# Four chunks of each layer's input weights, split by DMA and ScalarE in place of ScalarE and VectorE

## The chip, the cores and the metric

The kernel runs on one core of a Trainium2 chip. The metric is the device time of one execution in microseconds (us). In the text PE is TensorE, DVE is VectorE, ACT is ScalarE, POOL is GpSimd and SP is SyncE; us counts from the start of the profile's span.

## The reference

Two layers of a hybrid encoder over 512 tokens of width 1024, in float32, and a final RMSNorm.

```python
D_MODEL = 1024; SEQ = 512; DEPTH = 2
D_IN = 4 * NA_W + 4 * DIL_W + 3 * CONV_CH        # 3712 = 29 x 128
def hybrid_layer(x, g, w_in, rpb, w_dw, b_dw, ln_g, ln_b, w_pw, b_pw, w_out, pos):
    h = rms_norm(x, g)
    z = h @ w_in
    aq, ak, av, ag, bq, bk, bv, bg, ca, cb, cg = jnp.split(z, splits, axis=-1)
    ya = neighbourhood_attention(heads(aq), heads(ak), heads(av), rpb) * silu(ag)
    yb = dilated_attention(rotary(heads(bq)), rotary(heads(bk)), heads(bv)) * silu(bg)
    yc = conformer_conv(ca, cb, w_dw, b_dw, ln_g, ln_b, w_pw, b_pw) * silu(cg)
    return x + concatenate([ya, yb, yc]) @ w_out
```

What the change touches is the product h @ w_in: how the weights get on chip in the form that it wants.

## The kernel before

**Products in three parts.** Each float32 factor is split into a high part rounded to fp32r and a low part, the remainder. A product is a_hi w_hi + a_hi w_lo + a_lo w_hi, so three matmuls of 128x128 by 512 for each slice of 128 of the contraction. One 128-wide column tile of the weights is a chunk: [128, 8, 128], 512 KB, 24 matmuls (`products`, L476 to L490).

**Chunks.** A layer has 40 chunks: 29 of w_in in the order of IN_TILES (L47), 3 of w_pw with 3 slices only, 8 of w_out. Chunks 0 to 8 (PRE = 9, L56) come before the attention units, namely cb0, bq0, ca0, bk0, cb1, ca1, bq1, cb2, bk1; "cb", "ca" are the convolution's inputs, "bq", "bk" the queries and keys that get rotary embedding. From chunk 9 on, PE does half a chunk in each of the 40 attention units (an eighth of a pair of heads each), beside their scores, transpositions and value products. w_hi and w_lo have SPL = 5 slots; chunk c lies in slot c % 5, which is free when tile c - 5 is done.

**Two ways to get w_hi and w_lo.** `by_engines(c)` (L68) chooses.

- By engines (before: chunks 0 to 8): SP loads the chunk raw into one of 4 buffers inside pT (`load`, L387), ACT copies it to w_hi, which rounds (`split_hi`, L702), DVE subtracts w_hi from the raw chunk into w_lo (`split_weights`, L1202). PE waits for lo_ready.
- By transfers (all others): POOL issues a load that casts into w_hi (`load_hi`, L915), ACT writes the negative of w_hi to w_lo (`negate`, L695), and POOL issues the same load again with an adding transfer onto w_lo (`load_lo`, L921), so that w_lo = w - w_hi. PE waits for the semaphore of that transfer.

In the text a "casting load" is `load_hi`, an "adding load" is `load_lo`, and a pair is one of each.

**The order on the engines.** Everything is written out by hand. While PE works on chunk c, POOL issues the casting load of chunk c + 4 (`hi_next`, CAST_AHEAD) and the adding load of c + 3 (`lo_next`, AHEAD), ACT splits or negates chunk c + 3 (`split_next`), DVE splits c + 3 (`weights_next`), SP loads raw chunk c + 7 (`load_next`). An engine that waits holds up all that is queued behind it.

**Rotary.** For tiles bq and bk DVE writes the scaled tile to zs (in sq), SP swaps its halves with four small DMAs of 64 KB each (`swap`, L407, the "swap" of the text; swap 0 is chunk 1's, swap 1 chunk 3's, swap 2 chunk 6's), POOL multiplies by the sines (`rotate`, L950), DVE adds (`rotated`, L1080), ACT rounds q_hi or k_hi (L778), DVE makes q_lo or k_lo. On POOL `rotate` of chunk c - 1's tile stands behind `hi_next` and `lo_next` of step c (L967 to L971).

**The norm.** The RMS factor comes late: column sums on PE (L547), mean on DVE, the reciprocal root on POOL (`root`, L945), spread by PE (L556). The first tile is emptied only then.

**The units.** In unit n ACT does: empty the transposed tile of unit n - 3 (L787), exponential of unit n (L762), scaling of n - 1 (L769), and for even n `split_next`. PE's transposition of unit n - 2 (L590) waits until ACT has emptied the one before (pt_ready).

```python
for n in range(SLOTS):
    if n > LAG:
        empty_turn(l, n - LAG - 1)
    if n < UNITS:
        exps(l, n)
    if 0 < n <= UNITS:
        norm(l, n - 1)
    if n < UNITS:
        if n % 2 == 0:
            split_next(l, tile_at(n)[0])
```

Of the kernel before, what the change touches and what calls it, by code (L numbers as in the profile page):

```python
# [55 lines left out]
PRE = 9  # L56
# [3 lines left out]
SPL = 5  # L60
RAW = 4
AHEAD = SPL - 2
CAST_AHEAD = SPL - 1
RAW_AHEAD = AHEAD + RAW
# [1 line left out]


def by_engines(c):  # L68
    return c < PRE


PAIRS = 5
# [52 lines left out]
def build(nc, xT, w_in, w_pw, w_out, prm, gfin, nabias, lncnt, rope, out):  # L125
    with ExitStack() as ctx:
# [161 lines left out]
        def nth(l, c):  # L288

            return sum(by_engines(d % N_CH) == by_engines(c) for d in range(N_CH * l + c + 1))  # L290
# [4 lines left out]
        def follows(l, c):  # L295

            l, c = (l, c) if c < N_CH else (l + 1, c - N_CH)
            return (l, c) if l < DEPTH else None
# [11 lines left out]
        def emptied(l, c):  # L310

            return ACC0 + N_CH * l + c + 1
# [12 lines left out]
        def rope_of(c):  # L325
            kind, j = IN_TILES[c]
            return 2 * j + (kind == "bk") if kind in ("bq", "bk") else None
# [22 lines left out]
        def tile_at(n):  # L350

            return PRE + n // 2, n % 2 == 1
# [17 lines left out]
        def blocks(g):  # L370
            return (u if g else cs)[:, :, :].rearrange("p j t -> p (j t)")
# [13 lines left out]
        @block.sync  # L385
        def _(sp):
            def load(l, c):  # L387
                m = nth(l, c) - 1
                if l and c < RAW:

                    sp.wait_ge(tile_done, N_CH * (l - 1) + N_IN + CT + c + 1)
                elif m == RAW:
                    sp.wait_ge(w0_lo, len(W0_PARTS))
                elif m > RAW:
                    sp.wait_ge(lo_ready, m - RAW)
                sp.dma_start(raw[:, m % RAW, :, :], w_in[l, c]).then_inc(raw_in[m % RAW], 16)

            def load_next(l, c):
                f = follows(l, c + RAW_AHEAD)
                if f is not None and by_engines(f[1]):  # L400
                    load(*f)

            def load_first(i):
                part = slice(*W0_PARTS[i])
                sp.dma_start(raw[:, 0, part, :], w_in[0, 0][:, part, :]).then_inc(w0_in[i // 2], 16)

            def swap(l, r):  # L407

                sp.wait_ge(acc_free, emptied(l, IN_TILES.index(("bk" if r % 2 else "bq", r // 2))))
                for h in range(4):  # L410
                    o = 32 * (h ^ 1)
                    sp.dma_start(zsw[32 * h:32 * h + 32, :], zs[o:o + 32, :]).then_inc(swap_in, 16)

            def move_x(g, first, end):
                ks = list(X_BLOCKS.values())[g]
                sp.wait_ge(x_blocks, ks[-1] + 1)
                to = x[:, ks[0]:ks[-1] + 1, :].rearrange("p k (a t) -> p (k a) t", t=P)
                turned = blocks(g)[:, 0:len(ks) * SEQ].rearrange("p (b t) -> p b t", t=P)
                for i, j in QUADS[first:end]:
                    sp.dma_start(to[32 * j:32 * j + 32, :, 32 * i:32 * i + 32],  # L420
                                 turned[32 * i:32 * i + 32, :, 32 * j:32 * j + 32]).then_inc(x_moved, 16)

            def load_bias(l, un):
                b = un - DUNITS

                sp.wait_ge(m_ready, UNITS * l + (un - 1 if b >= 2 else DUNITS - 4))
                sp.dma_start(bias[:, b % 2, :], nabias[l, b]).then_inc(bias_in[b % 2], 16)

            sp.dma_start(par[:, :], prm[0]).then_inc(par_in, 16)
            for i, k in enumerate(K_ORDER):  # L430
                if i in W0_PARTS:
                    load_first(i)
                sp.dma_start(x[:, k, :], xT[:, k, :]).then_inc(x_in[k], 16)
            load(0, 1)
            load(0, 2)
            sp.dma_start(cs[:, :, :], rope).then_inc(const_in, 16)
            load(0, 3)
            sp.dma_start(cnt[:, :], lncnt).then_inc(const_in, 16)
            for c in range(RAW, RAW_AHEAD):
                load(0, c)  # L440
            for l in range(DEPTH):
                for c in range(PRE):
                    if (r := rope_of(c)) is not None:
                        swap(l, r)
                    load_next(l, c)
                if l == LAST:
                    sp.dma_start(gf[:, :], gfin).then_inc(gf_in, 16)
                for n in range(UNITS):
                    c, ends = tile_at(n)
                    if ends and (r := rope_of(c)) is not None:  # L450
                        swap(l, r)
                    if n == DUNITS - 4:
                        load_bias(l, DUNITS)
                        load_bias(l, DUNITS + 1)
                    if DUNITS <= n < UNITS - 2:
                        load_bias(l, n + 2)
                    if l == LAST and n in X_MOVES:
                        move_x(*X_MOVES[n])
                if l == LAST:
                    move_x(2, 2 * (UNITS - 37), len(QUADS))  # L460
                if l + 1 < DEPTH:

                    sp.wait_ge(ylo_ready, KD * (l + 1))
                    sp.dma_start(par[:, :], prm[l + 1]).then_inc(par_in, 16)
                for c in range(N_IN, N_CH):
                    load_next(l, c)
            for a in range(QT):
                sp.wait_ge(res_act, a + 1)
                sp.wait_ge(res_dve, a + 1)
                sp.dma_start(out[a, :, :], res[:, 2 * a:2 * a + 2, :]).then_inc(out_in, 16)  # L470
            sp.wait_ge(out_in, 16 * QT)
# [442 lines left out]
        def _(pool):  # L914
            def load_hi(l, c):  # L915
                src, K = chunk_src(l, c)
                if N_CH * l + c >= SPL:
                    pool.wait_ge(tile_done, N_CH * l + c - SPL + 1)
                pool.dma_start(w_hi[:, c % SPL, 0:K, :], src).then_inc(whi_in[c % SPL], 16)  # L919
# [6 lines left out]
            def hi_next(l, c):  # L926
                f = follows(l, c + CAST_AHEAD)
                if f is not None and not by_engines(f[1]):
                    load_hi(*f)

            def lo_next(l, c):
                f = follows(l, c + AHEAD)
                if f is not None and not by_engines(f[1]):
                    load_lo(*f)
# [10 lines left out]
            def root(l, k):  # L945

                pool.wait_ge(misc_free, MISC_L * l + k + 1)
                nc.gpsimd.tensor_tensor(rcol[:, :], col[:, :], nhalf[:, :], ALU.pow).then_inc(pow_ready, 1)
# [11 lines left out]
                                    pattern=[[-1, P]], channel_multiplier=1).then_inc(consts, 1)  # L960
            for l in range(DEPTH):
                if l == 0:
                    pool.wait_ge(const_in, 32)
                else:
                    add_squares(l, KD - 1)
                root(l, MISC_COL)
                for c in range(PRE):  # L967
                    hi_next(l, c)
                    lo_next(l, c)
                    if c and (r := rope_of(c - 1)) is not None:  # L970
                        rotate(l, r)  # L971
                for n in range(UNITS + 1):
                    if n < UNITS and n % 2 == 0:
                        hi_next(l, tile_at(n)[0])
                    if n < UNITS and n % 2 == 1:
                        lo_next(l, tile_at(n)[0])
                    if n % 2 and (r := rope_of(tile_at(n - 2)[0])) is not None:
                        rotate(l, r)
                    if n == LN_SUM:

                        pool.wait_ge(conv_step, STEPS * (l + 1))
                        for j in range(1, CT):
                            a = y[:, KD - CT, :] if j == 1 else ssq[:, :]
                            nc.gpsimd.tensor_tensor(ssq[:, :], a, y[:, KD - CT + j, :], ALU.add).then_inc(add_done, 1)
                            pool.wait_ge(add_done, ADD_L * l + KD - 1 + j)
                    if n == LN_MEAN + 1:
                        for j in range(1, CT):
                            add_squares(l, j, base=1)
                    if n == LN_BC - 2:
                        root(l, MISC_LCOL)  # L990
                for c in range(N_IN, N_CH):
                    hi_next(l, c)
                    lo_next(l, c)
                    if c >= N_IN + CT + 2 and l < LAST:
                        add_squares(l + 1, c - (N_IN + CT) - 1)
# [448 lines left out]
```

## Time and profile before

| what | value |
|---|---|
| median of 3 runs | 542.46 us (540.92 to 544.98) |
| the profiled execution | 542.2 us, of which the span of the profile is 540.2 us |
| PE busy | 528.5 us (98%) |
| DVE, ACT, POOL busy | 361.1, 287.3, 135.3 us |
| instructions | 7426 |
| DMA traffic | 86.26 MB, mean 160 GB/s |

The span goes from the first instruction to the last; the 2.0 us around it are the start and the end of the execution. Busy shares are means over the whole span. PE's matmuls overlap in the records, so a matmul "lasts" 390 ns but the next starts 227 ns after it.

### The profile page before, as it was taken

What the parts mean: (1) busy time and instruction counts of PE and PEld (TensorE: products, weight loads), DVE (VectorE), ACT (ScalarE), POOL (GpSimd) and SP (SyncE); (2) the same over time, 40 slices, a digit from 0 to 9 for tenths busy, and PEclk for the clock granted to TensorE, in tenths of its full rate; (3) what the DMA queues carried; (4) which work ended last, traced back from release to release, by engine and by line L of the source; (5) the groups of instructions that cost most, each with busy time, mean ns of one, the idle gap of its engine ahead of it and who ended that gap; (6) DMA issues with size and microseconds to landing.
All of it is one profiled execution on the core that took longest, in us unless ns stands there. A gap on an engine that the chain in (4) does not pass through costs nothing.

```text
span 540.2 us, 7426 instructions
## 1 busy us (share of the span) xinstructions
PE 528.5 (98%) x2684; PEld 416.0 (77%) x2684; DVE 361.1 (67%) x708; ACT 287.3 (53%) x546; POOL 135.3 (25%) x168
## 2 busy tenths in 40 slices
PE   7999999999999999999999999999999999999995
PEld 5788778687686888888888887877868778888884
DVE  5699798989773465521547959979999446554034
ACT  6433267667575566632533325856757566664223
POOL 0003232121132421333511223122111342223201
PEclk9999999999999999999999999999999999999999
DMA  8725687756474773799513369865595769689953
GB/s 263 280 75 133 147 188 181 165 128 152 103 163 110 161 184 69 177 246 306 142 36 99 102 133 225 204 136 131 141 175 122 178 130 207 126 163 235 227 88 157
DMA packets 47284, 86.26 MB, mean 160 GB/s; under 512 B 21264, under 2 KB 27280, under 8 KB 47248
## 3 DMA queue, kind: packets, MB, share of 16 engines
q0 software_dynamic: 17856, 61.09, 51.3%
q1 hardware_dynamic: 29392, 24.70, 15.5%
q8 instruction: 22, 0.36, 0.3%
q14 instruction: 14, 0.11, 0.1%
HBM read 78.43 MB, written 2.10 MB: 149 GB/s over the span
## 4 chain that ended last, share of the span: by engine, by line
PE 91%; DMA 4%; DVE 1%; ACT 1%; issue 1%; SPq 1%; POOL 1%; POOLq 0%; ACTq 0%
PE acc L484 21%; PE acc L486 20%; PE acc L485 20%; PE tp L590 5%; PE sc L576 5%; PE misc L618 4%; DMA w_hi<-w_in 2%; PE misc L624 1%; PE sc L528 1%; PE sc L484 1%; PE sc L486 1%; PE sc L485 1%; PE sc L529 1%; PE sc L530 1%; DMA sq<-sq 1%; PE misc L605 1%
## 5 line engine op out<-in xcount | busy, mean ns | idle before, releaser
L484 PE MATMUL acc<-act_hi,w_hi 128*128 128x512 f32 x496 | 202.5, 408 | 2.8 <-DVE act_lo L1221 2.6
L486 PE MATMUL acc<-act_lo,w_hi 128*128 128x512 f32 x496 | 194.2, 392 | 0.0
L485 PE MATMUL acc<-act_hi,w_lo 128*128 128x512 f32 x496 | 193.6, 390 | 0.0
L484 PEld LDWEIGHTS acc<-act_hi,w_hi 128*128 128x128 f32 x496 | 93.2, 188 | 28.4 <-issue 5.2
L486 PEld LDWEIGHTS acc<-act_lo,w_hi 128*128 128x128 f32 x496 | 93.1, 188 | 20.6
L485 PEld LDWEIGHTS acc<-act_hi,w_lo 128*128 128x128 f32 x496 | 93.4, 188 | 17.4 <-issue 0.5
L699 ACT ACTIVATE w_lo<-w_hi 128x1024 fp32r<-128x1024 f32 (+1 forms) x62 | 61.9, 998 | 48.0 <-DMA w_hi<-w_out 42.2
L762 ACT ACTIVATE prob<-prob,nmx 128x512 f32<-128x512 f32 (+1 forms) x80 | 50.6, 632 | 41.8 <-DVE nmx L1140 41.8
L787 ACT ACTIVATE pT<-tp 128x512 f32<-128x512 f32 (+1 forms) x80 | 40.6, 507 | 53.2 <-PE tp L590 52.8
L1120 DVE SCALAR_TENSOR_TENSOR y<-u,par,y 128x512 f32<-128x512 f32 x90 | 68.8, 764 | 0.0
L1120 DVE SCALAR_TENSOR_TENSOR acc<-u,par,acc 128x512 f32<-128x512 f32 x84 | 63.5, 756 | 0.0
L924 POOL DMA_DIRECT2D w_lo<-w_in x40 | 35.5, 888 | 94.5 <-ACT w_lo L699 94.3
L769 ACT ACTIVATE prob<-prob,rden 128x512 f32<-128x512 f32 (+1 forms) x80 | 50.2, 628 | 10.9 <-DVE rden L1146 10.6
L590 PEld LDWEIGHTS tp<-ident,prob 128*128 128x128 f32 x256 | 32.0, 139 | 15.3 <-issue 6.1
L590 PE MATMUL tp<-ident,prob 128*128 128x128 f32 x256 | 41.4, 274 | 0.5 <-ACT pT L787 0.5
L919 POOL DMA_DIRECT2D w_hi<-w_in x40 | 24.7, 617 | 59.3 <-PE acc L486 56.7
L952 POOL TENSOR_TENSOR sq<-sq,cs 128x512 f32<-128x512 f32 x12 | 17.4, 1449 | 74.8 <-DMA sq<-sq 74.8
L1140 DVE CUSTOM_DVE_ANT_0 prob<-sc,cnt 128x512 f32<-128x512 f32 x48 | 31.1, 685 | 6.0 <-PE sc L576 6.0
L1140 DVE CUSTOM_DVE_ANT_0 prob<-sc,bias 128x256 f32<-128x256 f32 x32 | 12.8, 422 | 28.7 <-PE sc L576 15.3
L924 POOL DMA_DIRECT2D w_lo<-w_out x16 | 14.0, 873 | 49.7 <-ACT w_lo L699 49.7
L1199 DVE TENSOR_TENSOR w_lo<-pT,w_hi 128x1024 fp32r<-128x1024 f32 (+2 forms) x20 | 23.0, 1156 | 4.3 <-ACT w_hi L708 2.6
L854 ACT ACTIVATE u<-u 128x512 f32<-128x512 f32 x6 | 3.8, 634 | 39.5 <-DVE u L1025 39.5
(139 smaller groups left out, 717.8 us busy)
## 6 DMA issues: line engine op xcount, KB each, us to landing
w_hi<-w_in POOLq DMA_DIRECT2D x40, 512.0 KB, 4.1
w_lo<-w_in POOLq DMA_DIRECT2D x40, 512.0 KB, 5.7
pT<-w_in SPq DMA_DIRECT2D x17, 512.0 KB, 5.1
w_hi<-w_out POOLq DMA_DIRECT2D x16, 512.0 KB, 7.5
w_lo<-w_out POOLq DMA_DIRECT2D x16, 512.0 KB, 6.5
bias<-nabias SPq DMA_DIRECT2D x32, 128.0 KB, 3.2
sq<-sq SPq DMA_DIRECT2D x48, 64.0 KB, 2.8
x<-xT SPq DMA_DIRECT2D x8, 256.0 KB, 6.1
```

The lines of the kernel that those rows point to most:

```text
L484: nc.tensor.matmul(to[:, :], w_hi[:, slot, k, :], a_hi[:, k, :], start=i == 0, stop=False)
L485: nc.tensor.matmul(to[:, :], w_lo[:, slot, k, :], a_hi[:, k, :], start=False, stop=False)
L486: last = nc.tensor.matmul(to[:, :], w_hi[:, slot, k, :], a_lo[:, k, :], start=False, stop=i == K - 1)
L576: last = nc.tensor.matmul(sc[2 * (b % 2) + h][:, 0:w], q[own, g % 2, b * P:(b + 1) * P], k[own, g % 2, first:first + w], start=i == 0, sto ...
L590: last = nc.tensor.transpose(tp[:, k * P:(k + 1) * P], prob[:, n % PROBS, k * P:(k + 1) * P], ident[:, :])
L699: nc.scalar.activation(w_lo[:, c % SPL, 0:K, :], w_hi[:, c % SPL, 0:K, :].bitcast(F32), ACT.Copy, scale=-1.0).then_inc(neg_ready, 1)
L762: nc.scalar.activation(prob[:, n % PROBS, 0:w], prob[:, n % PROBS, 0:w], ACT.Exp, scale=-1.0, bias=nmx[:, n % 4:n % 4 + 1], accum_out=den[ ...
L769: nc.scalar.activation(prob[:, n % PROBS, 0:w], prob[:, n % PROBS, 0:w], ACT.Copy, scale=rden[:, n % 4:n % 4 + 1]).then_inc(p_ready, 1)
L787: nc.scalar.activation(pT[:, h, 0:kk, b * P:(b + 1) * P], tp[:, 0:kk * P].rearrange("p (k t) -> p k t", t=P), ACT.Copy).then_inc(pt_ready, 1)
L924: pool.dma_start(w_lo[:, c % SPL, 0:K, :], src, accum_op=ALU.add).then_inc(wlo_in[c % SPL], 16)
L1120: ins = nc.vector.scalar_tensor_tensor(out=dst, in0=src, scalar=w, in1=dst, op0=ALU.mult, op1=ALU.add)
L1140: nc.vector.tensor_tensor_reduce(out=prob[:, n % PROBS, 0:w], in0=sc[n % 4][:, 0:w], in1=add, scale=-1.0, scalar=3e38, op0=ALU.add, op1=AL ...
```

## The change

`by_engines` is true for chunks 0 to 4 of a layer in place of 0 to 8. Chunks 5 to 8 are now split by transfers. In layer 0 SP's first raw loads end with chunk 4, and POOL issues the casting load of chunk 5 of layer 0 ahead of the reciprocal root.

```diff
 def by_engines(c):
-    return c < PRE
+    return c < SPL
@@ SP
-            for c in range(RAW, RAW_AHEAD):
+            for c in range(RAW, SPL):
                 load(0, c)
@@ POOL
             for l in range(DEPTH):
                 if l == 0:
+                    hi_next(0, 1)
                     pool.wait_ge(const_in, 32)
                 else:
                     add_squares(l, KD - 1)
                 root(l, MISC_COL)
                 for c in range(PRE):
-                    hi_next(l, c)
+                    if (l, c) != (0, 1):
+                        hi_next(l, c)
                     lo_next(l, c)
```

POOL's program at the start of layer 0, from the end of the constants on. L919 is the casting load, L924 the adding load, L948 the root, L952 a rotation; in brackets the semaphore that the instruction waits for. Before:

```order
L948 TENSOR_TENSOR rcol<-col,nhalf 128x4 [waits misc_free,const_in]
L952 TENSOR_TENSOR sq<-sq,cs 128x512 [waits swap_in] x2
L919 DMA w_hi<-w_in 128x1024 [waits tile_done] x2
L924 DMA w_lo<-w_in 128x1024 [waits neg_ready]
L919 DMA w_hi<-w_in 128x1024 [waits tile_done]
L924 DMA w_lo<-w_in 128x1024 [waits neg_ready]
```

And the same place in the changed kernel:

```order
L919 DMA w_hi<-w_in 128x1024 [waits tile_done]
L948 TENSOR_TENSOR rcol<-col,nhalf 128x4 [waits misc_free,const_in]
L919 DMA w_hi<-w_in 128x1024 [waits tile_done]
L924 DMA w_lo<-w_in 128x1024 [waits neg_ready]
L952 TENSOR_TENSOR sq<-sq,cs 128x512 [waits swap_in]
L919 DMA w_hi<-w_in 128x1024 [waits tile_done]
L924 DMA w_lo<-w_in 128x1024 [waits neg_ready]
L919 DMA w_hi<-w_in 128x1024 [waits tile_done]
L924 DMA w_lo<-w_in 128x1024 [waits neg_ready]
L952 TENSOR_TENSOR sq<-sq,cs 128x512 [waits swap_in]
```

The casting load of chunk 5 stands ahead of the root; the first rotation now has a pair of loads in front of it, the second two more pairs.

ACT's program from layer 0's first tanh (L854) on, as the difference. L708 is the copy of a raw chunk to w_hi, L699 the negative of a chunk that a transfer brought:

```order
 L854 ACTIVATE u<-u 128x512 [waits acc_free]
 L708 ACTIVATE w_hi<-pT 128x1024 [waits raw_in0]
-L708 ACTIVATE w_hi<-pT 128x1024 [waits raw_in1,tile_done]
-L708 ACTIVATE w_hi<-pT 128x1024 [waits raw_in2,tile_done]
-L778 ACTIVATE q_hi<-zc 128x512 [waits zc_ready]
-L708 ACTIVATE w_hi<-pT 128x1024 [waits raw_in3,tile_done]
-L854 ACTIVATE u<-u 128x512 [waits acc_free]
-L708 ACTIVATE w_hi<-pT 128x1024 [waits raw_in0,tile_done]
+L699 ACTIVATE w_lo<-w_hi 128x1024 [waits whi_in0]
+L699 ACTIVATE w_lo<-w_hi 128x1024 [waits whi_in1]
+L778 ACTIVATE q_hi<-zc 128x512 [waits zc_ready]
+L699 ACTIVATE w_lo<-w_hi 128x1024 [waits whi_in2]
```

Four copies have become four negatives in the same places, each waiting for a casting load in place of a raw load and a free slot. DVE loses four subtractions (L1199, 128x1024) in each layer, SP four raw loads; PE's program is the same.

## Rows read from the trace of the kernel before

**Rows 1.** The page's busy times: engine, busy us, share of the span, instructions.

```profile
PE 528.5 (98%) x2684; PEld 416.0 (77%) x2684; DVE 361.1 (67%) x708; ACT 287.3 (53%) x546; POOL 135.3 (25%) x168
```

**Rows 2.** By stretches: start:end, length, busy us (instructions) of PE, PEld, DVE, ACT, POOL; PE's clock, DMA share, GB/s.

```profile
30.00:62.00 32.00, 32.00 (x143) 26.39 (x141) 27.86 (x38) 9.34 (x12) 8.16 (x9) 1.00 0.49 124
62.00:80.00 18.00, 18.00 (x93) 14.07 (x92) 17.93 (x37) 9.95 (x20) 6.35 (x8) 1.00 0.77 174
284.00:323.00 39.00, 39.00 (x176) 32.06 (x176) 30.79 (x42) 10.88 (x13) 8.15 (x8) 1.00 0.45 116
323.00:341.00 18.00, 17.53 (x90) 13.58 (x91) 17.71 (x36) 9.51 (x19) 6.46 (x9) 1.00 0.93 212
```

**Rows 3.** Timeline of PE, layer 0: first matmuls of chunks 5 and 8.

```profile
40.35 0.39 PE L484 MATMUL acc<-act_hi,w_hi 128*128 128x512 f32 x1
...
56.67 0.39 PE L484 MATMUL acc<-act_hi,w_hi 128*128 128x512 f32 x1
```

**Rows 4.** Groups by form: line, engine, operation, count | busy us, mean ns | idle before.

```profile
L699 ACT ACTIVATE w_lo<-w_hi 128x1024 fp32r<-128x1024 f32 x56 | 58.8, 1050 | 48.0 <-DMA w_hi<-w_out 42.2 <-DMA w_hi<-w_in 5.7
...
L924 POOL DMA_DIRECT2D w_lo<-w_in x40 | 35.5, 888 | 94.5 <-ACT w_lo L699 94.3 <-issue 0.2
...
L919 POOL DMA_DIRECT2D w_hi<-w_in x40 | 24.7, 617 | 59.3 <-PE acc L486 56.7 <-issue 2.6
...
L1199 DVE TENSOR_TENSOR w_lo<-pT,w_hi 128x1024 fp32r<-128x1024 f32 x17 | 21.5, 1269 | 2.6 <-ACT w_hi L708 2.6
...
L708 ACT ACTIVATE w_hi<-pT 128x1024 fp32r<-128x1024 f32 x17 | 17.4, 1044 | 0.0
```

**Rows 5.** Timeline of POOL: start us, us, what, idle before and its releaser.

```profile
23.93 1.03 POOL L948 TENSOR_TENSOR rcol<-col,nhalf 128x4 f32<-128x4 f32 x1 [22.13 <-DVE col L1016]
33.10 1.29 POOL L952 TENSOR_TENSOR sq<-sq,cs 128x512 f32<-128x512 f32 x1 [8.14 <-DMA sq<-sq]
41.56 1.71 POOL L952 TENSOR_TENSOR sq<-sq,cs 128x512 f32<-128x512 f32 x1 [7.17 <-DMA sq<-sq]
...
52.23 0.92 POOL L924 DMA_DIRECT2D w_lo<-w_in  x1
...
312.85 0.91 POOL L924 DMA_DIRECT2D w_lo<-w_in  x1
```

**Rows 6.** The page's DMA queues: packets, MB, share of 16 engines' span.

```profile
q0 software_dynamic: 17856, 61.09, 51.3%
q1 hardware_dynamic: 29392, 24.70, 15.5%
```

**Rows 7.** Casting load by itself, L919 in 302 to 304 us.

```profile
DMA to landing us min/median/max: 3.6/3.6/3.6
```

**Rows 8.** Adding load by itself, L924 in 48 to 50 us.

```profile
DMA to landing us min/median/max: 6.6/6.6/6.6
```

**Rows 9.** Adding load between two casting loads, L924 in 62 to 63 us.

```profile
DMA to landing us min/median/max: 9.0/9.0/9.0
```

**Rows 10.** Swap by itself, L412 in 37 to 41 us.

```profile
DMA to landing us min/median/max: 1.9/2.0/2.0
```

**Rows 11.** The chain of waits, 312 to 340 us: start us, us, what.

```profile
314.60 7.23 DMA sq<-sq
...
324.29 10.55 DMA w_hi<-w_in
```

**Rows 12.** Timeline of ACT in layer 0: the copies of chunks 4, 5 and 6.

```profile
29.00 2.94 ACT L708 ACTIVATE w_hi<-pT 128x1024 fp32r<-128x1024 f32 x3
```

**Rows 13.** Timeline of ACT and of PE at the second transposition, layer 1.

```profile
335.83 0.58 ACT L787 ACTIVATE pT<-tp 128x512 f32<-128x512 f32 x1
...
336.55 0.63 PE L590 MATMUL tp<-ident,prob 128*128 128x128 f32 x4 [0.47 <-ACT pT L787]
```

**Rows 14.** Timeline of ACT and of PE at the second transposition, layer 0.

```profile
74.14 0.58 ACT L787 ACTIVATE pT<-tp 128x512 f32<-128x512 f32 x1
...
75.30 0.60 PE L590 MATMUL tp<-ident,prob 128*128 128x128 f32 x4
```

## The prediction

> **What bounds the kernel now.** I read the page's busy times first [rows 1]: TensorE (PE) is busy for 98% of the span, so what matters is where it stands idle. The table by stretches [rows 2] shows the two places where the change acts: 30 to 62 us (chunks 3 to 8 of layer 0) and 284 to 323 us (chunks 2 to 8 of layer 1). In both PE is busy for the whole stretch, 32.00 of 32.00 and 39.00 of 39.00 us. PE waits neither for a weight nor for a bank there, so an engine that is relieved in these stretches gives nothing back. Behind them there is one gap: 323 to 341 us has PE busy for 17.53 of 18.00 us. So the most that can be won is about half a microsecond, and the question is whether the change puts a wait where none is. PE's clock is 1.00 of full speed in all these rows (its 2.4 GHz level), and a stall of a few us leaves it alone in what I forecast.
>
> PE takes chunks in steps of 24 matmuls of 0.227 us, 5.44 us each; chunk 5 of layer 0 starts at 40.35 us and chunk 8 at 56.67 us [rows 3]. These are the due times of the weights.
>
> **What goes.** Eight raw loads of 512 KB on SP's queue, eight ScalarE copies (1044 ns) and eight VectorE subtractions (1269 ns) [rows 4]. VectorE wins 8 x 1.27 = 10.2 us, four subtractions in each layer. It is not waited for by PE in these stretches, so this counts 0; it is cover for the rotated sums, which now may come 1 to 2 us late without anything else moving.
>
> **What comes.** Eight casting loads and eight adding loads on GpSimd's queue, and eight ScalarE negatives. The negative takes 1050 ns where the copy took 1044 [rows 4]: 0. The issues cost GpSimd 8 x (0.62 + 0.89) = 12 us over both layers; nobody waits for GpSimd's time itself, only for its order: 0. GpSimd works in order, though, and so each rotation (12 in all) now stands behind an adding load, which waits for a negative, which waits for a casting load. The early issue of chunk 5 in layer 0 waits for tile 0, which is done at least four chunk times before 40.35, by 18.6 us. It stands ahead of the reciprocal root, which starts at 23.93 when its column has come [rows 5], so it delays nothing: 0.
>
> **The transfers.** This is the cost that counts. Queue q0 holds 56 full pairs and 6 small ones (3/8 of one): 58.25 pairs in 51.3% of 540.2 us, so 4.76 us of all 16 engines for a pair. Queue q1 moves 24.70 MB in 15.5%, so a raw chunk of 0.524 MB costs 1.78 us [rows 6]. The transfers of 30 to 62 us are busy 0.49 x 32 = 15.7 us [rows 2]. Of the four new pairs (19.0 us) chunks 5 and 6 have their casting halves (some 2.2 us each) before 30 us; one raw chunk (1.8) leaves. 15.7 + 19.0 - 4.4 - 1.8 = 28.5 us of 32: 89% busy. In 284 to 323 us: 0.45 x 39 = 17.6, less two raw chunks (3.6), plus 19.0 = 33.0 of 39, 85%. They still fit, but alone in the queue they no longer are. The latencies at both ends: a casting load 3.6 us by itself and 10.5 behind others, an adding load 6.6 and 9.0, a swap 2.0 and 7.2 [rows 7 to 11].
>
> **The schedule of layer 0, worked out from these.** ScalarE reaches chunk 4's copy at 29.00 us [rows 12]. Chunk 5's negative follows at 30.0, the adding load at 31.1, landed at 31.1 + 6.6 = 37.7; PE wants it at 40.35. The rotation of q0 waits for its swap until 33.1 as now [rows 5], so the adding load in front of it has just gone. Then come chunk 7's casting load (34.4), chunk 6's adding load (35.0, landed with 9.0 at 44.0, due 45.8) and chunk 8's casting load (35.6, with 10.5 at 46). Swap 1 falls among them and lands at about 44 to 45 instead of 41.5 [rows 5]; VectorE's three saved subtractions cover that. Chunk 7's adding load goes at 40.7 and lands at about 49 (due 51.2), chunk 8's at 47.6 and about 55.5 (due 56.7). Margins 2.6, 1.8, 2.2 and 1.2 us: all hold, none is wide. Take crowded values everywhere and each of chunks 6 to 8 is late by 1 to 2 us. For a wait of PE on a new adding load I therefore take 0, with bounds of 0 and +9 us (six chunks by 1.5).
>
> In layer 1 the norm comes earlier against PE and the raw loads that made swap 0 slow are gone, so the same four adding loads have 3 to 5 us.
>
> A rule bears on swap 1. Alone a swap lands in 2.0 us, among three POOL loads in 7.2 [rows 10, 11]. The Trainium skill (DMA: Bandwidth & Descriptors, "Queues, rings and completion order") says that each engine takes turns packet by packet between the rows with work, so a short transfer of SP's row should pay about its own time again. By that rule swap 1 would land by some 42.5 us, nothing behind it would move, and the sum would be the own time, 542.2. The trace's 7.2 us against 2.0 does not agree with it, so the sum goes by the row.
>
> **Where it shows.** What the lag does later is seen at chunk 13. Its casting load is issued at the first unit. ScalarE has to negate it before it empties the first transposed tile, and PE's second transposition waits for that. In layer 1 the load took 10.55 us [rows 11], the emptying started at 335.83 and PE's transposition came after a wait at 336.55 [rows 13]: the one stall. In layer 0 the emptying ended at 74.14 + 0.58 = 74.72 and the transposition started at 75.30 [rows 14]: 0.6 us of cover. With the change chunk 10's adding load is issued about 58 us instead of 52.2 in layer 0 and at about 315.6 instead of 312.9 in layer 1 [rows 5], and is still under way when chunks 12, 11 and 13 are issued. It holds them up by at most its half pair, 2.4 us. Layer 0: taken 1.8 us later, less 0.6 of cover, +1.2 us. Layer 1: taken 1.0 us later with no cover, +1.0 us. Bounds for each: 0 (even -0.5 in layer 1, if the queue happens to be emptier) and +3.
>
> **The sum.** 0 (VectorE) + 0 (ScalarE) + 0 (issues) + 0 (adding loads, 0 to +9) + 1.2 + 1.0 = +2.2 us. The profiled execution took 542.2 us (span 540.2 and 2.0 around it); the median of the runs is 542.46, so the same execution will do: 544.4 us.
>
> **The rivals.**
> Rival 1, late weights: the margins above are not there. Each chunk's pair has four chunk times, 21.8 us, from the release of its slot to its use. Crowded it wants 10.5 + 1.05 + 0.9 + 9.0 = 21.5 us, and any wait of GpSimd for a swap comes on top. The place is PE's first matmul of chunks 6, 7 and 8 in both layers; it decides once swap 1 holds GpSimd longer than about 1 us past my dates. Price 6 x 1.5 = 9 us beside +1 for chunk 13: 542.2 + 10 = 552. For it: 89% of the transfer time is taken, and the rows of 62 to 80 us [rows 2] show 0.77 with every latency at its crowded end. Against it: chunks 9 to 13 run the same way now and are in time.
>
> Rival 2, nothing: the queue has drained when chunk 13 is issued. The cover of 0.6 us holds in layer 0, the stall in layer 1 stays: 542.2. For it: GpSimd gets to chunk 12 only after swap 2, which lands at 321.8 us in layer 1 now [rows 11] and need not come later.
>
> Rival 3, a small gain: VectorE is ahead by several us when the units start, rotations and swaps come sooner, and the stall before 336.55 goes: 542.2 - 0.5 = 541.7. More isn't to be had, since PE has no other gap.
>
> **How the numbers follow.** Forecast 0.45 (about 544.4), rival 1 0.18 (552, with milder forms from 548), rival 2 0.27 (542.2), rival 3 0.10 (541.7). 1% is 5.4 us and about what a measurement of this kernel tells from no change. Faster by over 1% would take more than PE's whole idle time in these stretches: 0.01. Slower by over 1% (above 547.9) is rival 1 and a doubled forecast: 0.17. The rest, 0.82, is within 1%. The range runs from 541.2 to 549.5: below are only the runs' own scatter, above the worse half of rival 1.
>
> **What would show it.** Right: PE stays at 32.00 of 32 us up to the first scores, the transfers' share rises from about 0.5 to about 0.85 in both stretches, swap 1 lands several us after its issue, and PE's second transposition of both layers waits 1 to 2 us for ScalarE. VectorE's busy time falls by about 10 us. Wrong: a wait of PE (L484) for an adding load of chunks 5 to 8, which is rival 1; or no wait at 75 us and the old 0.5 us at 336, which is rival 2. If PE waits for a bank instead (VectorE held by a rotated sum), my cover of three subtractions was wrong.

## The result and the profile after

The changed kernel takes 543.82 us (median of 20 runs, 541.95 to 546.11), the kernel before 542.25 us beside it (20 runs): ratio 1.0034, 95% interval 1.0021 to 1.0047. It is slower by 1.6 to 1.8 us, and that is clear of the runs' scatter. Its profiled execution took 544.6 us with a span of 542.8 us. The time around the span is 1.8 us here and 2.0 before.

The table by stretches, as in [rows 2]: start:end, length, busy us of PE, PEld, DVE, ACT, POOL, then clock, DMA share, GB/s.

```profile
30.00:62.00 32.00, 32.00 (x143) 26.50 (x142) 22.85 (x34) 8.89 (x11) 10.75 (x13) 1.00 0.87 194
62.00:80.00 18.00, 17.21 (x89) 13.06 (x88) 16.36 (x31) 9.77 (x17) 8.00 (x9) 1.00 0.79 181
284.00:323.00 39.00, 38.02 (x170) 31.16 (x169) 25.73 (x38) 10.24 (x12) 11.08 (x15) 1.00 0.74 175
323.00:341.00 18.00, 18.00 (x93) 13.99 (x92) 15.32 (x29) 9.47 (x18) 8.21 (x10) 1.00 0.98 231
```

VectorE is relieved (27.86 to 22.85 us in the first stretch, 30.79 to 25.73 in the third) and PE has nothing of it. The transfers' share rises from 0.49 to 0.87 and from 0.45 to 0.74. PE's idle time stands in two places, and the old gap behind 323 us isn't there in this execution. The queues, as in [rows 6]:

```profile
q0 software_dynamic: 20160, 69.48, 57.9%
q1 hardware_dynamic: 28240, 20.51, 13.1%
```

The waits of PE: who waited for whom, us in total, times, longest.

```profile
PE acc L484 <- DMA w_lo<-w_in: 1.0, 1, 1.0
PE tp L590 <- ACT pT L787: 0.8, 1, 0.8
```

The second one is the second transposition of layer 0. The timelines of ACT and of PE there, as in [rows 14]:

```profile
74.84 1.06 ACT L699 ACTIVATE w_lo<-w_hi 128x1024 fp32r<-128x1024 f32 x1 [0.64 <-DMA w_hi<-w_in]
75.81 0.58 ACT L787 ACTIVATE pT<-tp 128x512 f32<-128x512 f32 x1
...
76.53 0.63 PE L590 MATMUL tp<-ident,prob 128*128 128x128 f32 x4 [0.79 <-ACT pT L787]
```

The first is chunk 8 in layer 1. GpSimd's timeline up to it, as in [rows 5], and the chain of waits there (start, us, what):

```profile
296.62 1.28 POOL L952 TENSOR_TENSOR sq<-sq,cs 128x512 f32<-128x512 f32 x1 [5.45 <-DMA sq<-sq]
297.85 0.59 POOL L919 DMA_DIRECT2D w_hi<-w_in  x1
298.43 0.92 POOL L924 DMA_DIRECT2D w_lo<-w_in  x1
298.99 0.91 POOL L919 DMA_DIRECT2D w_hi<-w_in  x1
303.37 0.86 POOL L924 DMA_DIRECT2D w_lo<-w_in  x1 [3.47 <-ACT w_lo L699]
```

```profile
301.54 7.62 DMA sq<-sq
309.16 0.07 issue
309.24 1.29 POOL sq L952
310.53 0.54 POOL w_hi L919
311.07 8.49 DMA w_lo<-w_in
319.56 0.04 issue
319.60 0.50 PE acc L484
```

Swap 1 is issued among three loads and takes 7.62 us. GpSimd stands in front of its rotation until 309.24. Then chunk 8's adding load goes, 8.49 us more, and PE has stood for 1.0 us at the chunk's first matmul. Every link is a wait of some engine, or of a transfer's issue, for the one before it.

A third part of the cost lies where PE has nothing to do any more. ScalarE's last instruction (L818) starts at 536.22 us before and at 538.29 now; the span ends 3.98 and 4.51 us later. The store of the last output behind it lands in the same 2.6 us, so 0.5 us more pass after the output is in place. This term is steady: 3.95 to 4.03 us in every profile of a kernel with 18 raw chunks, 4.2 to 4.3 with the change in one layer, 4.45 with six of the eight chunks changed and 4.5 to 4.6 with all eight. So it goes with the number of pairs that transfers bring, some 0.07 us for each, and with nothing else that the experiments below change. What the chip does there isn't shown. In this execution, then: 1.8 us of waits less the old 0.5, and 0.5 at the end.

PE's start differs between executions by more than 1 us: the third step of chunk 0 begins at 10.51 us in the profile before and anywhere from 9.45 to 10.90 in the others. So below I compare PE's gaps inside a profile, and medians for the time, never single spans. Points of time of different profiles are also shifted against each other: the column sums of layer 1's first norm (L547) start at 280.5 us before, 281.7 in the changed kernel, 280.9 in e2_layer1 and 279.6 to 279.9 in e3_chunk8_raw, e5_rot_first and e6_rot_dve. One measure is free of that: from the column sums of layer 0's first norm to those of layer 1's last, PE takes 419.46 us before and 421.24 in the changed kernel.

### The profile page after: what moved, and what is told of

It is laid out like the page before. It is cut to its first block, busy times and chain, and to the rows that moved or that the text cites. A ratio compares the mean times of both kernels' runs of the same rounds, so it can differ in the third digit from the quotient of the medians.

```text
span 542.8 us, 7418 instructions
## 1 busy us (share of the span) xinstructions
PE 529.2 (97%) x2684; PEld 416.0 (77%) x2684; DVE 351.4 (65%) x700; ACT 288.1 (53%) x546; POOL 145.1 (27%) x184
## 3 DMA queue, kind: packets, MB, share of 16 engines
q0 software_dynamic: 20160, 69.48, 57.9%
## 4 chain that ended last, share of the span: by engine, by line
PE 80%; DMA 9%; DVE 3%; SPq 2%; issue 2%; POOL 1%; ACT 1%; POOLq 0%; DVEq 0%; ACTq 0%
PE acc L484 19%; PE acc L486 18%; PE acc L485 18%; PE tp L590 5%; DMA sq<-sq 5%; PE sc L576 5%; PE misc L618 4%; DMA w_hi<-w_in 2%; SPq L412 2%; DMA w_lo<-w_in 2%; PE misc L624 1%; PE sc L528 1%; PE sc L530 1%; PE sc L529 1%; PE misc L605 1%
## 5 line engine op out<-in xcount | busy, mean ns | idle before, releaser
L484 PE MATMUL acc<-act_hi,w_hi 128*128 128x512 f32 x496 | 202.6, 408 | 3.7 <-DVE act_lo L1223 2.6
L484 PEld LDWEIGHTS acc<-act_hi,w_hi 128*128 128x128 f32 x496 | 93.2, 188 | 30.0 <-issue 5.8
L699 ACT ACTIVATE w_lo<-w_hi 128x1024 fp32r<-128x1024 f32 (+1 forms) x70 | 70.3, 1006 | 75.5 <-DMA w_hi<-w_out 39.6
L924 POOL DMA_DIRECT2D w_lo<-w_in x48 | 42.3, 882 | 126.7 <-ACT w_lo L699 126.6
L919 POOL DMA_DIRECT2D w_hi<-w_in x48 | 31.0, 646 | 63.9 <-PE acc L486 63.0
L952 POOL TENSOR_TENSOR sq<-sq,cs 128x512 f32<-128x512 f32 x12 | 16.2, 1346 | 46.4 <-DMA sq<-sq 46.4
L924 POOL DMA_DIRECT2D w_lo<-w_out x16 | 13.8, 863 | 48.0 <-ACT w_lo L699 48.0
L1087 DVE TENSOR_TENSOR zc<-zc,sq 128x512 f32<-128x512 f32 x12 | 8.2, 686 | 25.8 <-POOL sq L952 25.8
L1153 DVE SCALAR_TENSOR_TENSOR y<-th,y 128x512 f32<-128x512 f32 x22 | 15.1, 686 | 12.4 <-ACT th L756 12.3
```

The source lines that it names most:

```text
L484: nc.tensor.matmul(to[:, :], w_hi[:, slot, k, :], a_hi[:, k, :], start=i == 0, stop=False)
L699: nc.scalar.activation(w_lo[:, c % SPL, 0:K, :], w_hi[:, c % SPL, 0:K, :].bitcast(F32), ACT.Copy, scale=-1.0).then_inc(neg_ready, 1)
L924: pool.dma_start(w_lo[:, c % SPL, 0:K, :], src, accum_op=ALU.add).then_inc(wlo_in[c % SPL], 16)
```

## The experiments

Theory A, formed on this profile: the cost is two waits of PE, at the second transposition (chunk 13's negative is late) and at chunk 8 of layer 1 (its adding load is late), and behind both stands GpSimd's order: it waits for a slow swap with loads queued behind. Rivals: B, the cost is spread over many small slow-downs; C, a lag that all chunks share; D, the amount of transfers counts and the order doesn't.

### e1_layer0 and e2_layer1: the change in one layer alone

```diff
-def by_engines(c):
-    return c < SPL
+def by_engines(c, l=0):
+    return c < (5, 9)[l]
```

The calls pass the layer on; e2_layer1 has (9, 5).

> The change in layer 0 alone; layer 1 takes chunks 0 to 8 raw as before. Theory A (two places): PE waits some 0.9 us at the second transposition near 75 us, nothing at chunk 8 of layer 1, and the old 0.5 us near 337 us is there again: 542.3 + 0.9 = 543.2 us, +0.9. Theory B (the cost is spread, because VectorE and GpSimd or the transfers slow each other everywhere): half of the whole cost, +0.8, without a gap of PE that accounts for it.

> The change in layer 1 alone. Theory A: no gap near 75 us; PE waits about 1.1 us at chunk 8's first matmul of layer 1 (near 317 us) and the 0.5 us near 337 us is gone: +0.6 us. Theory B: +0.8 us with no gap at chunk 8.

Layer 0 alone: 542.05 us against 541.89, ratio 1.0003 (0.9987 to 1.0018): nothing. Its profile has no wait near 75 us, and none near 337 us although layer 1 is as before, so both places that A named for it are empty; 1.3 us of waits stand at the last value products (L624), a place that the change doesn't touch and where e2_layer1 and e9_before_late have some too. Layer 1 alone: 543.16 us, ratio 1.0025 (1.0009 to 1.0041), +1.3 us. PE's waits in its profile:

```profile
PE tp L590 <- ACT pT L787: 1.6, 1, 1.6
PE misc L624 <- ACT pT L787: 0.7, 1, 0.7
```

The 1.6 us are the second transposition of layer 1; chunk 8 lost only 0.2 us there (its first matmul at 317.85; the last of chunk 7 at 317.41 and 0.23 us make 317.64). So A had the layer's cost too low and the place wrong in this execution: PE waits for chunk 13's negative and hardly for chunk 8. By the medians most of the cost lies in layer 1, 1.3 of 1.6 us, and layer 0 has 0.2 of it; the intervals (-0.7 to +1.0 and +0.5 to +2.2 us) leave room for another split. The 0.8 us of layer 0 in the profile above are not in this one. B fares no better than A by the times, since +0.8 lies in both intervals. What speaks against it is that PE's 1.6 us at one wait make up most of layer 1's cost in the profile.

### e3_chunk8_raw: chunks 5 to 7 alone

```diff
 def by_engines(c):
-    return c < SPL
+    return c < SPL or c == 8
```

> The change for chunks 5 to 7 only; chunk 8 stays raw in both layers, so one pair of loads less in each stretch and no adding load behind swap 1. Theory A: swap 1 of layer 1 lands at about 306 instead of 309 us, PE does not wait at chunk 8, and the wait near 75 us falls from 0.9 to 0.3 us or none: +0.3 us at most. If the lateness of chunk 8 is only a sign of a lag that all chunks share (theory C), chunk 7 or 9 waits in its place and the cost stays near +1.5 us.

A miss: 545.51 us, ratio 1.0058 (1.0035 to 1.0081), +3.6 us, with less moved by transfers than in the changed kernel. Chunk 8 does not wait, as A said, and swap 1 lands at 305.8, as it said too. But swap 2 lands at 323.7 (321.8 before), chunk 13's casting load goes at 326.1 and lands at 336.1, and the wait at the second transposition is the longest of all. PE's timeline there and the stretches behind it (start:end, length, busy, clock, DMA share, GB/s):

```profile
337.80 0.63 PE L590 MATMUL tp<-ident,prob 128*128 128x128 f32 x4 [2.19 <-ACT pT L787]
```

```profile
334.00:338.00 4.00, 1.81 (x9) 1.20 (x9) 3.97 (x9) 3.32 (x6) 1.74 (x2) 1.00 0.99 238
...
338.50:342.00 3.50, 3.50 (x14) 2.37 (x15) 3.50 (x9) 1.33 (x3) 1.48 (x3) 0.51 0.88 194
```

Behind a stall of 2.19 us the granted clock is 0.51 of full speed over 3.5 us, which loses 1.7 us. Stall and clock together, less the old 0.5 us, are 3.4 of the 3.6. Four of its seven runs have a mean clock of 0.993 or 0.994 over the span, where 29 of the 30 of the kernel before beside them have 0.996 or more; so the clock probably fell in those four. Taking a pair of loads away did not help, which speaks against D. For C it speaks in part: the lateness that chunk 8 lost turned up at chunk 13. Why swap 2 took 6.4 to 7.7 us a piece and came later than before, though a pair of loads was gone, was not followed up.

### e4_late_neg: ScalarE empties first and negates after

```diff
                     if n > LAG:
                         empty_turn(l, n - LAG - 1)
+                    if n == LAG + 1:
+                        split_next(l, tile_at(2)[0])
...
-                        if n % 2 == 0:
+                        if n % 2 == 0 and n != 2:
                             split_next(l, tile_at(n)[0])
```

> The changed kernel, with one edit: ScalarE negates chunk 13 after it has emptied the first transposed tile instead of before. Theory A: the 0.9 us near 75 us is gone, chunk 8's wait of 1.1 us in layer 1 stays: 543.8 - 0.9 = 542.9 us, +0.6 against the kernel before. If the casting load of chunk 13 was not what PE waited for, the gap near 75 us stays.

543.12 us, ratio 1.0018 (0.9994 to 1.0042): between no gain and all of it, inconclusive as a time. Its profile shows the mechanism. In layer 1 chunk 13's casting load is as late as ever, and ScalarE's emptying no longer waits for it:

```profile
334.01 0.58 ACT L787 ACTIVATE pT<-tp 128x512 f32<-128x512 f32 x1
334.88 1.06 ACT L699 ACTIVATE w_lo<-w_hi 128x1024 fp32r<-128x1024 f32 x1 [0.30 <-DMA w_hi<-w_in]
```

PE transposes at 335.12 without a wait. 0.4 us come back two transpositions later, at 343.87. The wait for chunk 8 that A said would stay isn't there in this execution. At the second transposition of layer 0 PE does not wait either, but neither does it in e1_layer0, without this edit.

### e5_rot_first: in layer 1 the first rotation ahead of chunk 5's adding load

```diff
                 for c in range(PRE):
...
-                    lo_next(l, c)
+                    if not (l and c == 2):
+                        lo_next(l, c)
                     if c and (r := rope_of(c - 1)) is not None:
                         rotate(l, r)
+                    if l and c == 2:
+                        lo_next(l, c)
```

> The changed kernel; in layer 1 GpSimd's rotation 0 stands ahead of chunk 5's adding load instead of behind it. Theory A (swap 0 of layer 1 is slow because that adding load is issued among its four pieces): swap 0 lands by itself, at about 292 us instead of 294 to 296; chunk 7's casting load goes 2 to 3 us earlier, chunk 8's adding load too, and PE's waits of layer 1 (1 to 2 us) shrink to 0 or 0.5: +0 to +0.5 us against the kernel before. Chunk 5's adding load itself goes later and lands about 300, due 302. Theory D (GpSimd's order does not matter, only the amount of transfers): swap 1 still lands near 307 us and the cost stays near +1.4 us.

542.86 us against 542.18, ratio 1.0016 (1.0003 to 1.0028): by the medians about half of the cost of the changed kernel, though the two intervals overlap. The rotation starts at 292.03 instead of 296.62, of which 1.8 us are the shift between the two profiles and 2.8 the edit:

```profile
292.03 1.34 POOL L952 TENSOR_TENSOR sq<-sq,cs 128x512 f32<-128x512 f32 x1 [7.42 <-DMA sq<-sq]
293.31 0.89 POOL L924 DMA_DIRECT2D w_lo<-w_in  x1
293.92 0.85 POOL L919 DMA_DIRECT2D w_hi<-w_in  x1
```

Swap 0 takes 2.0 to 2.7 us a piece here and 2.4 to 5.2 in the changed kernel, whose adding load stands among its pieces. Swap 1 is still crowded (landed 305.6), chunk 8 is in time, and 0.9 us of waiting remain at the second transposition. From norm to norm PE takes 419.84 us, against 421.24. The direction is A's; the time is a little above the +0 to +0.5 us that it gave.

### e6_rot_dve and e7_rot_late: GpSimd freed of the swaps

```diff
             def rotated(l, r):
-                dve.wait_ge(t2_ready, ROPES * l + r + 1)
+                dve.wait_ge(swap_in, 64 * (ROPES * l + r + 1))
+                nc.vector.tensor_tensor(zsw, zsw, cs[:, 1, :], ALU.mult).then_inc(t2_ready, 1)
+                dve.wait_ge(t2_ready, ROPES * l + r + 1)
                 dve.wait_ge(dve_own, own[0])
@@ POOL: rotate and both its calls are gone
```

> The changed kernel with the rotation's product (12 of 128x512) on VectorE, right before the sum, so that GpSimd never waits for a swap. Theory A (GpSimd, held by swaps, issues the loads late): casting loads go as soon as their slot is free, chunk 8's adding load of layer 1 at about 306 instead of 308 to 311, chunk 13's casting load at about 323.5 instead of 324.5 to 327.5, no wait of PE in either layer: -0.5 us to 0 against the kernel before, 541.5 us. Theory D (only the amount of transfers counts): more loads in flight at once, same landings, cost stays +1.4. VectorE's 12 x 0.69 = 8.3 us are less than the 10 that it was given.

> e6_rot_dve and e4_late_neg in one. Theory A: no wait of PE is left between 17 and 345 us; as e6_rot_dve, perhaps 0.3 us less: 541.4 us.

e6: 541.64 us, ratio 0.9995 (0.9983 to 1.0007). e7, with the edit of e4 as well: 541.82 us, 0.9993 (0.9979 to 1.0008). Neither is slower than the kernel before, with the same transfers as in the changed kernel. But the edit gains something on the kernel before too, so the fair comparison comes below, with e8 and e10. The stretches of e6:

```profile
30.00:62.00 32.00, 32.00 (x144) 26.25 (x144) 24.54 (x38) 9.83 (x12) 9.65 (x14) 1.00 0.99 222
62.00:80.00 18.00, 18.00 (x95) 14.19 (x92) 17.90 (x38) 10.87 (x20) 3.73 (x6) 1.00 0.82 187
284.00:323.00 39.00, 39.00 (x176) 32.05 (x176) 28.89 (x43) 11.47 (x14) 10.31 (x15) 1.00 0.88 208
323.00:341.00 18.00, 18.00 (x94) 14.21 (x91) 17.81 (x38) 11.19 (x22) 3.54 (x6) 1.00 0.88 215
```

The transfers are busier than in the changed kernel (0.99 and 0.88 against 0.87 and 0.74) and PE doesn't stand still once. This is what decides against D for the waits of PE: at 0.88 and 0.99 of the transfer engines' time PE has no wait, as long as GpSimd can issue when a slot comes free. GpSimd's timeline now has waits for PE and for ScalarE alone:

```profile
305.33 0.86 POOL L924 DMA_DIRECT2D w_lo<-w_in  x1 [3.12 <-ACT w_lo L699]
307.16 0.54 POOL L919 DMA_DIRECT2D w_hi<-w_in  x1 [0.96 <-issue]
```

305.33 is chunk 8's adding load (311.07 in the changed kernel, 309.3 with the shift of 1.8 us taken off); it lands at 311.4, over 5 us before chunk 8 starts. Swap 1 still has a piece of 5.3 us (landed 306.7), and VectorE has the slack to wait for it.

### e8_before_rot_late, e9_before_late, e10_before_rot: the same edits on the kernel before

The edits are those of e6 and e4: both (e8), the late negative alone (e9), the rotation on VectorE alone (e10).

> The kernel before with the same two edits as e7_rot_late; nine chunks arrive raw. VectorE has no slack of 10 us here: four subtractions per layer stay and 4.1 us of products per layer come on top. Theory A: the waits that the edits cure are at most the 0.5 us near 337 us, so -0.5 to 0 (541.6 us), unless VectorE, 27.9 of 32 us busy and now with 30, empties a bank late: then +1 or more. Comparison with e7_rot_late tells whether the raw chunks or the transfers are better once GpSimd is free.

> The kernel before, with chunk 13's negative behind the emptying of the first transposed tile, and nothing else. If the 1.1 us that e8_before_rot_late won come from this edit, this kernel wins them too: 541.1 us, -1 us. If they come from the rotations, it wins at most the 0.5 us near 337 us, -0.3 us.

> The kernel before, with the rotation's product on VectorE, and nothing else. If the rotations on GpSimd are what makes chunk 13's casting load late, it lands at about 327.5 instead of 333 to 335 us, the wait near 337 us is gone, and this kernel alone has the 1 us of e8_before_rot_late: 541.2 us. If both edits are needed, -0.5 us.

| kernel | median us | before beside it | ratio | interval |
|---|---|---|---|---|
| e8_before_rot_late | 541.13 | 542.18 | 0.9980 | 0.9968 to 0.9992 |
| e9_before_late | 541.14 | 541.37 | 0.9993 | 0.9981 to 1.0004 |
| e10_before_rot | 540.72 | 541.37 | 0.9984 | 0.9973 to 0.9995 |

The rotation edit is what gains: alone 0.16%, 0.7 us by the medians and 0.9 by the ratio. The late negative adds nothing that can be told by the time, though e9's profile too is without the 0.5 us near 337. In e10 the casting load of chunk 12, the adding load of chunk 11 and the casting load of chunk 13 go out 2 to 3 us apart, each when it can, where GpSimd sent all three at once behind swap 2 before:

```profile
317.33 0.54 POOL L919 DMA_DIRECT2D w_hi<-w_in  x1 [3.99 <-PE acc L486]
319.68 0.88 POOL L924 DMA_DIRECT2D w_lo<-w_in  x1 [1.81 <-ACT w_lo L699]
322.76 0.54 POOL L919 DMA_DIRECT2D w_hi<-w_in  x1 [2.21 <-PE acc L486]
```

Chunk 13's load lands 3.8 us later, at 326.6, instead of 10.5 us. e8 and e10 beat both kernels of this case, with nine raw chunks and VectorE at 32.27 of 39 us in e8's third stretch.

Now the fair comparison: what does the change cost when both kernels have the rotation on VectorE? e7 (five raw chunks) and e8 (nine) carry the same two edits and ran side by side, 12 times each: 541.82 against 541.13, so the change costs 0.7 us, and drawing again from the 24 times gives 0.2 to 1.6. So some of the cost is left, and the profiles say where. From norm to norm PE takes 418.78 us in e6, e8 and e10 and 418.83 in e7: in this part the change costs 0.05 us at most. But from ScalarE's last instruction to the end of the span it is 4.55 us in e6 and e7 against 4.00 in e10 and 3.95 in e8, the 0.5 us described above. For that term the amount of transfers does count, as D said.

### e11_hold: what a stall of PE costs

The kernel before, with three further negatives ahead of chunk 13's in layer 1, of the same values into the same place.

```diff
                 act.wait_ge(whi_in[c % SPL], landed(l, c))
+                for i in range(3 if (l, c) == (1, 13) else 0):
+                    nc.scalar.activation(w_lo[:, c % SPL, 0:K, :], w_hi[:, c % SPL, 0:K, :].bitcast(F32), ACT.Copy,
+                                         scale=-1.0).then_inc(held, 1)
+                    act.wait_ge(held, i + 1)
```

> The kernel before, with three more negatives of 1.05 us by ScalarE ahead of chunk 13's in layer 1 (same values into the same place), so PE's second transposition there waits some 3.5 us longer. It prices a stall of PE. If a stall costs its own length and no more: +3.3 us. If TensorE's granted clock falls to half after such a stall, as it did for 3.4 us behind the 2.2 us wait of e3_chunk8_raw, then about 1.5 us on top: +5 us, and the granted clock of 323 to 345 us is under 1.00.

546.08 us against 541.37, +4.7 us (ratio 1.0085, 1.0066 to 1.0104). PE's timeline behind the wait, and the stretches:

```profile
339.20 0.63 PE L591 MATMUL tp<-ident,prob 128*128 128x128 f32 x4 [3.74 <-ACT pT L792]
339.76 0.66 PE L577 MATMUL sc<-k_hi,q_hi 64*128 64x512 f32 x2
340.21 0.63 PE L577 MATMUL sc<-k_hi,q_lo 64*128 64x512 f32 x2
```

```profile
339.90:343.40 3.50, 3.50 (x14) 2.38 (x15) 2.10 (x7) 2.32 (x6) 0.41 (x1) 0.51 0.87 143
```

A clock of 0.51 over 3.5 us is a loss of 1.7 us. The stall is 3.7 us, 3.2 more than the 0.5 of [rows 13]; 3.2 + 1.7 = 4.9 for a measured 4.7. The second half of the expectation holds.

## Why the prediction was right, and where it was not

**The time and the direction** were right: 544.4 us forecast, +2.2 on the own time, and +1.6 to +1.8 measured. That the sum comes so near is partly luck: the term of layer 0 was too large, that of layer 1 about right by another wait in part, and 0.5 us at the end of the span are in no term. By its own signs the prediction did less well. PE waited 0.8 us at the second transposition of layer 0 and not at all at that of layer 1, where 1 to 2 us were forecast for each; and the wait for an adding load (L484), which it had named as a sign against it, came at chunk 8 of layer 1.

**What counted 0** did: VectorE's relief (9.7 us less busy, 361.1 to 351.4) bought nothing, ScalarE's negatives and GpSimd's issues cost nothing by themselves, the root at 24.21 instead of 23.93 delayed nobody.

**The transfers.** 89% forecast for 30 to 62 us and 87% measured; 85% for 284 to 323 us and 74%, a difference that wasn't followed up. A pair at 4.76 us: 57.9% of 542.8 us for 66.25 pairs is 4.74.

**The schedule of layer 0** came out to within 0.7 us for the adding loads. Adding loads of chunks 5 to 8: forecast to land at 37.7, 44.0, 49 and 55.5, landed at 37.1, 43.5, 48.3 and 56.1. Swap 1: forecast 44 to 45, landed 46.7. Chunk 13's casting load: forecast 1.8 us later, issued at 64.65 instead of 62.84.

**The term "layer 0, +1.2 us"** was too large as a median. The profile has a gap of the forecast kind (0.8 us), but the change in layer 0 alone measures +0.2 us (interval -0.7 to +1.0), and the profiles of e1, e4 and e5, where layer 0 is changed in the same way, show no gap there. I had taken the delay of chunk 13's casting load as fixed at 1.8 us. Counted from layer 0's column sums, it goes 1.5 us later than before in the changed kernel's profile, but 0.2, 0.3 and 1.4 us later in those of e1, e4 and e5. That fits rival 2 for this layer.

**The step that failed** is the sentence on layer 1: "the norm comes earlier against PE and the raw loads that made swap 0 slow are gone, so the same four adding loads have 3 to 5 us." The raw loads are gone, and chunk 5's adding load comes in their place, right among the pieces of swap 0. Counted from the column sums, the rotation behind swap 0 starts 2.0 us later than with the raw loads, GpSimd waits for it, and everything behind goes late. Of the 3 to 5 us chunk 8 had -1.1 (landed at 319.56, due at 318.24 + 0.23). e5_rot_first showed the link: with the adding load behind the rotation, that rotation starts 2.8 us earlier, chunk 8 is in time and PE's waits of layer 1 in the profile are 0.9 us. Layer 1's term was +1.0 and measured +1.3, by another wait in part: I had it at chunk 13 alone, and it falls on chunk 8 or on chunk 13 (2.2 us at one place in e3_chunk8_raw), as the execution goes. Some 0.3 us of this layer's cost are at the end of the span, where I had nothing.

**The rivals.** Rival 1 named the first wait at the right place (chunks 6 to 8, decided by how long a swap holds GpSimd) with 9 us for a price where one chunk of six was late by 1.0. Rival 3 had VectorE's lead bring rotations forward. It does not, since they wait for swaps, and those got slower.

**Swap 1 and the rule.** In this trace as in the one before, a swap among loads takes 7 us (6.9 to 7.6 here) where one by itself takes 2.0 [rows 10]. The Trainium skill (DMA: Bandwidth & Descriptors, "Queues, rings and completion order") has each engine take turns between the rows with work, packet by packet. It gives no time for a short transfer among long ones; that it should pay about its own time again was my reading. The runs don't agree with that reading, and the forecast that went by the row was the better one.

**What stays open**: what takes the 0.5 us at the end of the span, and why a swap among loads takes 7 us and not 4. No run changed the size or the number of its pieces. Nor was it tried whether another order of the pieces against the loads would do as well as moving the product to VectorE.

## What to carry to other kernels

An engine that issues transfers in order should not also wait for slow ones. Before giving it more loads, list what stands in front of each issue: here transfer engines that were 88 to 99% busy cost PE no wait once GpSimd waited for slots and negatives alone, and at 74 to 87% they cost waits of 1.8 us in one execution while it waited for swaps. Where PE had no idle time, relief of another engine bought nothing by itself, and the best use found was to take the blocking product off the issuing engine: that took the change from +0.34% to -0.05%, and the kernel before to -0.16%. Compare such a cure on both kernels. Here that shows that some 0.7 us of the change's cost are left, most of them behind the last output, where no look at waits finds them.

## What the runs showed of the hardware

After stalls of 2.2 us (e3_chunk8_raw) and 3.7 us (e11_hold) TensorE's granted clock was 0.51 over a stretch of 3.5 us, so nearly all of it at the 1.2 GHz level; the pairs of score matmuls followed each other at 0.43 us there, and 1.7 us were lost beyond the stall. Behind the stalls of 0.5 to 1.6 us in the other profiles it stayed at 1.00 (e2_layer1, whose stall was 1.6 us, has 1.00 from 338 to 346 us). The prediction had a stall of a few us leave the clock alone; a forecast that prices these two by their length alone is 1.7 us too low.

Between the last output and the end of the span, a kernel with eight more pairs brought by transfers takes 0.5 us more (4.51 against 3.98 us from ScalarE's last instruction on), and the experiments with four and six more lie in between (4.2 to 4.3 and 4.45).
